# Output gates' modulation blocks moved from the hyena branch products and w_out to the two convolutions of a hybrid diffusion block

## What is computed

```python
sh1, sc1, gt1, sh2, sc2, gt2 = modulation(c, w_mod, b_mod, 6)   # silu(c) @ w_mod + b_mod, six chunks of 1024
h = rmsnorm(x, g_norm1) * (1 + sc1) + sh1
... = h @ w_in                      # columns of the mixers, and three gates g_b of 1024
y_hy = hyena_mix(...)               # two long convolutions by FFT, one after the other
m = sigmoid(g_hy) * (y_hy @ w_br_hy) + sigmoid(g_gla) * (y_gla @ w_br_gla) + sigmoid(g_s5) * (y_s5 @ w_br_s5)
x = x + gt1 * (m @ w_out)
h2 = rmsnorm(x, g_norm2) * (1 + sc2) + sh2
x = x + gt2 * swiglu(h2, w_ffn_in, w_ffn_out)
return rmsnorm(x, g_final)
```

## Time and profile before

| | |
|---|---|
| median of 3 runs | 1220.83 us (1220.79 to 1224.56) |
| the profiled execution's own time | 1218.67 us |
| its span in the profile | 1216.8 us |
| mean granted TensorE clock | 0.953 |
| TensorE busy | 1112.2 us (91%) |
| VectorE busy | 585.7 us (48%) |
| ScalarE busy | 401.3 us (33%) |
| GpSimd busy | 335.1 us (28%) |

### The profile page before, as it was taken

How to read it: one execution, slowest core, us unless ns; L and a number is a source line. 1 busy time by engine, 2 the same in 40 slices (tenths; PEclk the granted TensorE clock), 3 DMA queues, 4 the chain that set the end, 5 groups by cost and what they waited for, 6 DMA issues and landing times.

```text
span 1216.8 us, 15749 instructions
## 1 busy us (share of the span) xinstructions
PE 1112.2 (91%) x6109; PEld 848.5 (70%) x6109; DVE 585.7 (48%) x1135; ACT 401.3 (33%) x763; POOL 335.1 (28%) x288
## 2 busy tenths in 40 slices
PE   4899989978989999998997979798999999999995
PEld 1478958866567676777473654697888888888884
DVE  3775156576489888783196965435000012000014
ACT  2762323443344534432411100234332212232221
POOL 2032213503100000000131210351655545665540
PEclk9889999989889998998998989899999999999998
DMA  9920223855223323323423227661333223333211
GB/s 315 277 97 32 69 69 130 135 150 169 67 64 87 88 70 72 86 58 98 147 87 121 69 101 260 195 182 42 104 104 104 64 94 104 102 104 104 80 42 70
DMA packets 139367, 134.32 MB, mean 110 GB/s; under 512 B 12937, under 2 KB 125865, under 8 KB 138268
## 3 DMA queue, kind: packets, MB, share of 16 engines
q1 hardware_dynamic: 126448, 105.52, 29.8%
q0 software_dynamic: 3744, 16.15, 3.6%
q10 hardware_dynamic: 9100, 11.64, 3.2%
HBM read 120.18 MB, written 11.01 MB: 108 GB/s over the span
## 4 chain that ended last, share of the span: by engine, by line
PE 72%; DVE 15%; ACT 4%; issue 4%; DMA 3%; ACTq 1%; POOL 0%; DVEq 0%; SPq 0%; POOLq 0%
PE psum L744 59%; DMA buf<-in_w_mod 2%; PE psum L1077 2%; PE psum L777 1%; PE psum L1004 1%; PE psum L1107 1%; PE psum L984 1%; DMA buf<-in_w_out 1%; PE psum L789 1%; DVE ring_lo L2054 1%; PE psum L882 1%; PE psum L808 1%; PE psum L997 1%; ACTq L1580 1%; DVE buf L2130 1%
## 5 line engine op out<-in xcount | busy, mean ns | idle before, releaser
L1296 POOL TENSOR_TENSOR ring_lo<-buf,ring_hi 128x512 fp32r<-128x512 f32 (+2 forms) x220 | 281.9, 1314 | 498.0 <-ACT ring_hi L1451 497.9
L744 PE MATMUL psum<-hT_hi,ring_hi 128*128 128x512 f32 x712 | 286.7, 403 | 8.7 <-DVE hT_lo L2393 4.0
L744 PE MATMUL psum<-hT_lo,ring_hi 128*128 128x512 f32 x712 | 279.9, 393 | 0.0
L744 PE MATMUL psum<-hT_hi,ring_lo 128*128 128x512 f32 x712 | 279.7, 393 | 0.0
L1451 ACT ACTIVATE ring_hi<-buf 128x512 fp32r<-128x512 f32 (+1 forms) x260 | 139.6, 610 | 224.2 <-PE psum L744 160.8
L744 PE MATMUL psum<-buf,buf 128*128 128x512 f32 (+1 forms) x368 | 153.5, 574 | 21.4 <-issue 15.4
L744 PEld LDWEIGHTS psum<-hT_hi,ring_hi 128*128 128x128 f32 x712 | 135.5, 190 | 42.6 <-issue 5.5
L744 PEld LDWEIGHTS psum<-hT_lo,ring_hi 128*128 128x128 f32 x712 | 135.9, 191 | 28.6 <-issue 1.7
L744 PEld LDWEIGHTS psum<-hT_hi,ring_lo 128*128 128x128 f32 x712 | 135.3, 190 | 29.1
L744 PEld LDWEIGHTS psum<-buf,buf 128*128 128x128 f32 x368 | 69.4, 208 | 94.3 <-issue 85.0
L2402 DVE TENSOR_TENSOR buf<-psum,buf 128x512 f32<-128x512 f32 x22 | 15.2, 692 | 220.7 <-PE psum L744 220.7
(11 more groups left out here) (333 smaller groups left out, 1705.8 us busy)
## 6 DMA issues: line engine op xcount, KB each, us to landing
buf<-in_w_in SPq DMA_DIRECT2D x26, 1024.0 KB, 5.3
buf<-in_w_mod SPq DMA_DIRECT2D x24, 1024.0 KB, 8.3
buf<-in_w_ffn_in SPq DMA_DIRECT2D x44, 512.0 KB, 5.2
buf<-in_w_ffn_out SPq DMA_DIRECT2D x8, 1024.0 KB, 5.1
scr_k<-buf POOLq DMA_DIRECT2D x4, 1024.0 KB, 5.5
buf<-scr_k POOLq DMA_DIRECT2D x4, 1024.0 KB, 7.9
buf<-in_w_out SPq DMA_DIRECT2D x4, 1024.0 KB, 6.6
buf<-in_w_ffn_out SPq DMA_DIRECT2D x4, 768.0 KB, 4.6
```

The lines of the kernel that those rows point to most:

```text
L744: ins = nc.tensor.matmul(o, a, b, start=start and n == 0, stop=stop and n == len(pairs) - 1)
L1296: nc.gpsimd.tensor_tensor(ring_lo[:, a:a + n], ring[:, a:a + n], ring_hi[:, h + i * n:h + i * n + n].bitcast(fp32), SUB)\
```

## The change

The order of the modulation blocks and broadcasts in the list of steps changes, and with it the order of the loads in the ring; every block's row now has a buffer of its own (`gate_row`: two old row buffers, three pieces of `restart`, three of the region at `par_at`), so that rows may wait for their broadcast. Block 8 is made before `uunfold(0)`, blocks 9, 10 and 11 before `yinv(0)`, block 20 after `ufold(1)`, blocks 21 and 22 before `yinv(1)`, block 23 beside the second hyena branch product. The broadcasts `gt` of 8, 9, 10, 11 and 20 stand beside the branch products, those of 21, 22, 23 before `wo(0)`. GpSimd issues the loads of the gate biases before the load of x, on a semaphore of their own; VectorE waits for that one before the first gate row, and for x before the first w_out product.

```diff
--- before.py
+++ after.py
@@ -291,6 +291,9 @@
         Lr, Li = (v3(r.take(9 * 32), 9) for _ in range(2))
         dtmp = r.take(GB * 16)[0:16, :]
         y_s5 = v3(at_words(U_at, 4 * L), 4)
+        gate_row = dict(zip((8, 9, 10, 11, 20, 21, 22, 23),
+                            mrow + [restart[:, k:k + 256] for k in (0, 256, 512)]
+                            + [at_words(par_at + 512 + 256 * k, 256) for k in range(3)]))
         G5 = oT
 
 
@@ -568,6 +571,13 @@
             step(*e)
         step("glu")
         one_beside()
+        gates = [8, 9, 10, 11, 20, 21, 22, 23]
+
+        def mod_gate():
+            i = gates.pop(0)
+            want(f"mod{i}", block(w_mod, 256 * i), split=False)
+            step("mod", i)
+
         for cv in range(2):
             step("uspec", cv, 1)
             step("uquart", cv)
@@ -575,6 +585,8 @@
             one_beside()
             step("ufold", cv)
             one_beside()
+            if cv:
+                mod_gate()
             for jt in range(2):
                 step("uhalf", cv, jt)
                 step("ufilt", cv, jt, 0)
@@ -582,40 +594,34 @@
                 step("ufilt", cv, jt, 1)
                 one_beside()
                 step("ucomb", cv, jt)
+            if cv == 0:
+                mod_gate()
             step("uunfold", cv)
             one_beside()
+            for _ in range((3, 2)[cv]):
+                mod_gate()
             step("yinv", cv)
             one_beside()
         while late or beside:
             one_beside()
             one_beside()
-        gates = [8, 9, 10, 11, 20, 21, 22, 23]
-        made = []
-
-        def mod_gate():
-            if gates:
-                i = gates.pop(0)
-                want(f"mod{i}", block(w_mod, 256 * i), split=False)
-                step("mod", i)
-                made.append(i)
-            if len(made) > 1 or not gates:
-                step("gt", made.pop(0))
-
         beside = ms0
+        rows_at = {2: (8,), 3: (9, 10), 4: (11,), 5: (20,)}
         for n in range(8):
             one_beside()
-            if n > 2:
+            if n == 1:
                 mod_gate()
+            for i in rows_at.get(n, ()):
+                step("gt", i)
         one_beside()
         step("mT_split")
+        for i in (21, 22, 23):
+            step("gt", i)
         for i in range(4):
             want(f"wo{i}", block(I["w_out"][0], 256 * i))
             step("wo", i)
-            mod_gate()
             if i == 0:
                 step("A2")
-        while made:
-            mod_gate()
         step("h2T")
         for hf in range(2):
             for j in range(hf * NFH, (hf + 1) * NFH):
@@ -796,7 +802,7 @@
                 evacuated(pe, f"mr{i}")
                 name = f"gt{i}"
                 o = open_job(name)
-                close(nc.tensor.matmul(o[:, 0:256], pick[:, 0:1].to_broadcast([P, P]), mrow[i % 2],
+                close(nc.tensor.matmul(o[:, 0:256], pick[:, 0:1].to_broadcast([P, P]), gate_row[i],
                                        start=True, stop=True), name)
 
             def h_T():
@@ -1357,9 +1363,9 @@
                             .then_inc(S("kept_sig"), 16)
                     pool.wait_ge(S("branch0"), 1)
                     ld = S("p4_load")
+                    pool.dma_start(bgt[0], I["b_mod"][0][2 * D:3 * D].partition_broadcast(P)).then_inc(S("gate_bias"), 16)
+                    pool.dma_start(bgt[1], I["b_mod"][0][5 * D:6 * D].partition_broadcast(P)).then_inc(S("gate_bias"), 16)
                     pool.dma_start(xr, I["x"][0].rearrange("(t p) d -> p t d", p=P)).then_inc(ld, 16)
-                    pool.dma_start(bgt[0], I["b_mod"][0][2 * D:3 * D].partition_broadcast(P)).then_inc(ld, 16)
-                    pool.dma_start(bgt[1], I["b_mod"][0][5 * D:6 * D].partition_broadcast(P)).then_inc(ld, 16)
                     pool.dma_start(gfin, I["g_final"].partition_broadcast(P)).then_inc(ld, 16)
 
             stages = dict(setup=setup, split=split, act_split=act_split, s5_load=s5_load, hy_tok=hy_tok,
@@ -1794,9 +1800,10 @@
                 if i >= 8 and i % 2 in last_T:
                     full(dve, last_T[i % 2])
                 o = full(dve, f"mr{i}")
-                V.tensor_copy(mrow8[i] if i < 8 else mrow[i % 2], o[:, 0:256]).then_inc(freed(f"mr{i}"), 1)
-                if i >= 8:
-                    last_T[i % 2] = f"mod{i}" if 12 <= i < 20 else f"gt{i}"
+                row = mrow8[i] if i < 8 else gate_row[i] if i in gate_row else mrow[i % 2]
+                V.tensor_copy(row, o[:, 0:256]).then_inc(freed(f"mr{i}"), 1)
+                if 12 <= i < 20:
+                    last_T[i % 2] = f"mod{i}"
 
             def mod_T(i):
                 if i < 8 and i % 4 != 3:
@@ -2352,7 +2359,7 @@
                 k = 0 if i < 12 else 1
                 c = 256 * (i - (8, 20)[k])
                 if i == 8:
-                    dve.wait_ge(S("p4_load"), 64)
+                    dve.wait_ge(S("gate_bias"), 32)
                 name = f"gt{i}"
                 o = full(dve, name)
                 V.tensor_tensor(gt[k][:, c:c + 256], o[:, 0:256], bgt[k][:, c:c + 256], ADD).then_inc(freed(name), 1)
@@ -2369,6 +2376,8 @@
                 for t in range(4):
                     name = f"wo{i}{t}"
                     o = full(dve, name)
+                    if i + t == 0:
+                        dve.wait_ge(S("p4_load"), 32)
                     c = slice(256 * i, 256 * i + 256)
                     V.tensor_tensor(xtmp[:, 0:256], o[:, 0:256], gt[0][:, c], MUL).then_inc(freed(name), 1)
                     evacuated(dve, name)
```

## The result

| | before | after |
|---|---|---|
| median | 1224.17 us (1220.48 to 1225.5, 7 runs) | 1230.28 us (1221.08 to 1232.16, 7 runs) |
| ratio to before, 95% interval | | 1.0065 (1.0046 to 1.0083) |
| profiled execution, span | 1218.67, 1216.8 us | 1229.49, 1227.7 us |
| TensorE busy | 1112.2 us | 1110.0 us |
| mean granted clock | 0.953 | 0.954 |

The change makes the kernel slower by 0.65%, 7.9 us on the 1220.83 of the first table (0.46 to 0.83%, that is 5.6 to 10.1 us; the medians above differ by 6.1 us, 0.50%). The forecast was 4.4 us slower (0.36%); the measured interval lies above it, inside the forecast's range. The direction was right, the size was not.

What follows compares the result with a forecast made beforehand. TensorE was taken as the bound, with 72% of the chain of waits. Terms 0 + 8.7 + 6.7 + 1.5 - 6.1 - 6.4 = +4.4 us on the median 1220.83 gave 1225.2 us, range 1216.5 to 1231.

Steps and rivals of the forecast that it cites:

- The blocks around the first convolution: Blocks 8 to 11 before the first inverse transform: 0 us, bounds -1.4 and +2.5.
- Block 20: Second convolution: its copy delays VectorE's chain and the second inverse transform, +8.7 us, bounds +7 and +10.
- Y: Start of the second inverse transform, 713.70 us in the kernel before; later times are counted from it.
- br00: First hyena branch weight block: lands late beside GpSimd's loads, TensorE stands still, +6.7 us, bounds 0 and 8.3.
- slow clock +1.5: Lower TensorE clock after the stall for the first hyena branch block: +1.5 us, bounds 0 and 3.
- From there to w_out: First hyena branch product to first w_out product: 35.9 us instead of 42.0, -6.1 us.
- The w_out products: Four products of 11.36 us, 45.4 instead of 51.85 us: -6.4 us.
- The chain from 826.71 to the end stays: Everything after the w_out products: claimed unchanged, 0 us.
- Biases: GpSimd's gate bias loads ahead of x: nothing waits for them, 0 us.
- br00 in time: Rival at the first hyena branch block: it lands in time, 1217.0 us; chance 0.20 with what lies near.
- The slow clock before block 20: Rival: lower clock also hits the stretch VectorE waits on, up to +2.5 us there, 1231 in all; chance 0.1.
- Equal turns: Rival: SP's and GpSimd's queues alternate packets, first branch block lands at Y + 23.3, 1222.6 us; outcomes 1219 to 1224.5 get 0.32.

Runs made afterwards that it cites:

- experiment 1: Changed kernel with VectorE's copy of block 20 moved behind the first filtering of the second convolution: 1218.66 us, ratio to the kernel before 0.9977.
- Experiment 2: Changed kernel with GpSimd issuing the biases, x and g_final only once the first hyena branch block has landed: 1223.48 us, ratio to before 1.0022.
- Kernel 5: kernel 3 with GpSimd's split of the second w_out block held until the eight merged rows are written: 1210.25 us, ratio to before 0.9925.
- experiment 4: Kernel before with only the gate biases loaded ahead of x, on their own semaphore: 1220.93 us, ratio to before 0.9998.
- kernel 8: Only the first convolution's half of the change: blocks 8 to 11 moved, 20 to 23 beside branch and w_out products: 1211.1 us, ratio to before 0.9931.
- 10: kernel 8 with GpSimd's split of the second w_out block held until the last merge: 1210.97 us, ratio to before 0.9923.
- kernel 3: Changed kernel with block 20's copy behind the first filtering and GpSimd's four loads behind the first branch block's landing: 1214.28 us, ratio to before 0.9931.
- 7: Changed kernel with block 20's copy behind the first filtering and blocks 22 and 23 between later branch products: 1213.69 us, ratio to before 0.9947.
- 9: Only the second convolution's half: blocks 20 to 23 as in the change, 8 to 11 beside branch products: 1234.5 us, ratio to before 1.0116.

## Why the prediction was wrong in size

Point by point, by its own steps:

- **The blocks around the first convolution, 0.** Right: +0.15 us, with the 3.3 us pause before block 11 that was forecast (3.47). The lower clock behind that pause took what the earlier start would have gained.
- **Block 20, +8.7.** Right: Y came 8.8 us later, `uhalf` at 685.5 without the 2.2 us of offset (forecast 685.6), and experiment 1 took 0.9 points back by moving that copy alone.
- **br00, +6.7 and slow clock +1.5.** Right in place and size. Forecast: requested at Y + 15.75, landed at Y + 25.9, TensorE idle for 6.7 us. Measured: Y + 15.2, Y + 25.1, 6.56 us. The clock's part was 2.0 us (8.87 against 6.87). Experiment 2 shows the cause: 3.42 us when GpSimd's loads wait.
- **From there to w_out, -6.1.** From Y on the sum was right within 0.4 us, in part by luck: the five gate rows took 0.43 us each and not 0.63, 1.0 us less, while the end was 4.9 us and not 4.25. And one part of it hid the error of the next term. The forecast let VectorE finish 2.75 us after the last product, plus 1.5 for collisions, and treated these as passing time. They hold a pause of TensorE: 1.30 us of gate rows, then 3.61 us of nothing.
- **The w_out products, -6.4: this is the step that failed.** "Four times 11.36" assumed the full clock, although the same text had used the row of 12.89 us after a pause to price the br00 stall. The pause before w_out did to the first w_out product what the earlier ones do: 0.50 until about 791 us. The products took 47.2 us instead of 45.4, so the term was -4.7. Kernel 5 has 45.7 with a pause of 1.52 us.
- **"The chain from 826.71 to the end stays".** The second failure, +1.0 us, put at nothing in the forecast. The first feed-forward split starts about 2.2 us behind the end of the third w_out product, before (815.93) as after (825.60). Before, a block and a gate row stood between the third and the fourth product, the split ended at 821.15, and the sum that the norm waits for began at 821.60 and took 0.42. After, they are gone, the split reaches 1.6 us further into the fourth product, and that sum takes 1.53. The other kernels agree: with a block and a row there the way from w_out to the feed-forward is 7.6 us (kernels 4, 8, 10), with neither 8.6 (1, 2, 3, 5, 7, 9). The collision was priced where the merges are and forgotten where the norm is.
- **Biases, 0.** Right (experiment 4).

In the profiles the change costs 6.8 us where the forecast had 4.4; the two mis-sized terms make 2.7 us of it, the rest -0.3. The timing's 7.9 (5.6 to 10.1) is 1.1 us more, which is within its interval and stays open.

Of the rivals, *br00 in time* did not happen. The slow clock before block 20 did come (0.50 from 651 to 653 us, 0.65 in the next two), but its cost was made up before block 20: +0.15 us. *Equal turns* is instructive. From 744 to 748 us the two queues do take turns, 157 packets beside 159 and 170 beside 172, as the Trainium skill's page "DMA: Bandwidth & Descriptors" has it in "Queues, rings and completion order". The trace agrees with the rule while both queues have data moving, and the time worked out from it, Y + 23.3, was wrong: SP's queue had moved no packet in the first 2 us after its issue and 18 in the next two, while GpSimd's moved 387. The count of 355 beside 795 is the mean of a start with nothing and an even sharing. Before, from 732 to 734 and from 734 to 736:

```profile
q0 software_dynamic: 186, 0.70, 96.5%
q1 hardware_dynamic: 46, 0.05, 8.8%
...
q0 software_dynamic: 136, 0.49, 72.9%
```

SP's queue moved 135 packets beside those 136. The slow start is not SP's alone: in kernel 3, where SP's loads were under way first, GpSimd's queue, first issued at 733.90, moved nothing until 737 us, while SP's moved 724 packets from 733 on. Nothing run here shows what holds the start back.

## What to carry to other kernels

An operation put into an idle stretch of one engine must be followed on every engine that it touches: here 1.0 us of matmul was free, and its 0.42 us copy stood in front of a VectorE chain with no slack, 9 us before its operand was ready. A load that is moved ahead in an in-order ring pushes back all that follow; find which of them now falls beside the largest other transfer, and ask it again after each repair, for the stall moves on to the next (here from br00 to br01 and wo0). And when a sum contains a pause of TensorE like these (3.2 to 6.6 us), price the matmuls behind it from a row that follows one. Last, try the halves of a change by themselves: here one half was a gain and the other a larger loss.

## What the runs showed of the hardware that was not expected

A VectorE operation with two operands in SBUF, put beside GpSimd's splits, is not only slowed to 1.6 to 1.8 us. It can stand still. After, GpSimd's split of four rows:

```profile
660.86 5.00 POOL L1302 TENSOR_TENSOR ring_lo<-buf,ring_hi 128x512 fp32r<-128x512 f32 x4
```

and VectorE beside it:

```profile
661.85 0.69 DVE L2188 TENSOR_TENSOR buf<-psum,buf 128x512 f32<-128x512 f32 x1 [0.34 <-DVE buf L2347]
662.69 3.73 DVE L2193 TENSOR_TENSOR buf<-buf,buf 128x512 f32<-128x512 f32 x1
```

The second merge operation, 0.69 us elsewhere, starts at 662.69 and lasts 3.73. The operation before it, which reads PSUM, takes its usual 0.69 inside the same split, and so do all operations from PSUM beside the split at 767.38. This agrees with the Trainium skill's page "SBUF — State Buffer", section "SBUF: two separate sides", by which a GpSimd operation that reads SBUF and a VectorE operation with two SBUF inputs exclude each other. The trace adds that the cast, with one input, is slowed too (1.38 for 0.43). That a single operation is held for 3.73 us, longer than one operation of the split (5.00 us for four), stays unexplained. So a merge's first operation is safe beside a split, and its other three are not.

A pause before w_out of 3.17 us was enough to find the clock at its lower level behind it (kernel 8: the first w_out product took 13.12 us, a later one 11.35); behind the 1.52 us of kernel 5 the granted clock stayed at 1.00, and so it did after the change behind the 1.91 us before 662.69. The pause alone does not decide: before, the clock was back at 0.50 from 656 to 658, behind a pause of only 2.31 us, which had another of 5.38 us shortly ahead of it.
